# Hybrid encoder trunk on one core: a buffer for each operand of the first head pair, its V products and the tables' products in another place, and roots and reciprocals of the norms on 16 turned columns

## What is computed

```python
def rmsnorm(x, g):
    y = xf * lax.rsqrt(jnp.mean(xf * xf, axis=-1, keepdims=True) + RMS_EPS)
    return (y * g.astype(jnp.float32)).astype(x.dtype)
...
def reference(x, ...):
    for layer in range(DEPTH):
        h = rmsnorm(x, attn_norm[layer])
        if layer % 2 == 0:
            x = x + even_mixer(h, even_w_in[i], na_rpb[i], even_w_out[i], t5_table)
        else:
            x = x + mla_mixer(h, odd_w_in[i], ...)
        h = rmsnorm(x, ffn_norm[layer])
        x = x + swiglu(h, ffn_w_gate[layer], ffn_w_up[layer], ffn_w_down[layer])
    return rmsnorm(x, final_norm)
```

## Time and profile before

| | us |
|---|---|
| median of three runs (lowest, highest) | 2806.12 (2805.36, 2809.89) |
| profiled execution | 2809.95 |
| its span | 2808.1 |
| TensorE busy | 2699.4 |
| DVE, POOL, ScalarE busy | 1757.6, 1435.2, 943.5 |
| mean granted clock of TensorE | 0.988 |

### The profile page before, as it was taken

The page is one execution under the profiler, slowest core; times in us unless marked ns, Lnnn a source line. Parts: engine busy times, 40 slices in busy tenths (PEclk is TensorE's granted clock), DMA queues, the critical chain, the costliest instruction groups (busy, mean ns, idle before and its releaser), DMA issues. The chain is left out here.

```text
span 2808.1 us, 41204 instructions
## 1 busy us (share of the span) xinstructions
PE 2699.4 (96%) x13500; PEld 2245.7 (80%) x13500; DVE 1757.6 (63%) x2843; ACT 943.5 (34%) x1746; POOL 1435.2 (51%) x1353
## 2 busy tenths in 40 slices
PE   6999999989999999999998999999999999999996
PEld 4888888878788887887767888888887788878875
DVE  5666666664855555555577777777566545555555
ACT  3555544562411000011235666666532001111002
POOL 2333344465656555656643333333766555665554
PEclk8999999999999999999999999999999999999998
DMA  5433334334312111111235333334432111111112
GB/s 163 109 95 91 85 77 106 90 123 138 90 46 60 52 45 49 52 56 45 69 96 138 97 88 99 92 87 142 136 98 61 49 49 60 45 57 55 45 45 75
DMA packets 273210, 228.43 MB, mean 81 GB/s; under 512 B 44585, under 2 KB 237473, under 8 KB 272897
## 3 DMA queue, kind: packets, MB, share of 16 engines
q1 hardware_dynamic: 271223, 222.16, 28.4%
q10 hardware_dynamic: 1859, 4.64, 0.5%
HBM read 158.06 MB, written 17.04 MB: 62 GB/s over the span
## 5 line engine op out<-in xcount | busy, mean ns | idle before, releaser
L773 POOL TENSOR_SCALAR xT<-xT,rden 128x1024 f32<-128x1024 f32 (+2 forms) x256 | 278.0, 1086 | 645.7 <-DVE rden L1898 645.7
L814 POOL TENSOR_TENSOR ring<-block_t,ring 128x512 fp32r<-128x512 f32 x312 | 411.0, 1317 | 24.9
L1176 PE MATMUL psS<-times_r,ring 128*128 128x512 f32 x928 | 366.6, 395 | 16.0 <-ACT rstd L1589 9.5
L812 POOL CAST ring<-block_t 128x512 fp32r<-128x512 f32 x312 | 208.8, 669 | 322.1 <-PE psD L1210 138.3
L1483 ACT ACTIVATE pt<-psD 128x512 fp32r<-128x512 f32 (+2 forms) x512 | 257.9, 557 | 337.5 <-PE psD L985 336.5
L1177 PE MATMUL psS<-times_r,ring 128*128 128x512 f32 x928 | 363.3, 391 | 0.0
L1178 PE MATMUL psS<-times_r,ring 128*128 128x512 f32 x928 | 363.1, 391 | 0.0
L1906 DVE TENSOR_TENSOR pt<-psD,pt 128x512 fp32r<-128x512 f32 (+2 forms) x512 | 303.8, 635 | 81.3 <-ACT pt L1483 80.7
L2097 DVE TENSOR_TENSOR xT<-psD,xT 128x512 f32<-128x512 f32 x320 | 218.8, 690 | 175.1 <-PE psD L1210 175.1
L1890 DVE CUSTOM_DVE_ANT_0 xT<-psS,xT 128x1024 f32<-128x1024 f32 (+2 forms) x256 | 287.5, 1123 | 4.3 <-PE psS L972 3.4
L1472 ACT ACTIVATE xT<-xT,mneg 128x1024 f32<-128x1024 f32 (+2 forms) x256 | 273.5, 1069 | 35.6 <-DVE mneg L1890 35.3
(11 more groups left out here) (288 smaller groups left out, 5005.2 us busy)
## 6 DMA issues: line engine op xcount, KB each, us to landing
block_t<-in_w_gate SPq DMA_DIRECT2D x96, 256.0 KB, 2.9
block_t<-in_w_up SPq DMA_DIRECT2D x96, 256.0 KB, 3.3
block_t<-in_w_down SPq DMA_DIRECT2D x88, 256.0 KB, 3.1
kq<-split_x SPq DMA_DIRECT2D x126, 128.0 KB, 2.4
kq<-row SPq DMA_DIRECT2D x126, 128.0 KB, 2.3
xT<-rel_c SPq DMA_DIRECT2D x16, 960.0 KB, 5.3
stage<-in_w_even SPq DMA_DIRECT2D x24, 512.0 KB, 3.8
heads<-o_out SPq DMA_DIRECT2D x128, 64.0 KB, 2.1
```

What stands on the lines that cost most here:

```text
L773: pool.tensor_scalar(s, s, rden[:, t % 4:t % 4 + 1], 1.0, ALU.mult, ALU.mult).then_inc(S["normed"], 1)
L814: pool.tensor_tensor(lo, src, hi.bitcast(F32), ALU.subtract).then_inc(S["ws"], 1)
L1176: pe.matmul(o, unit(u, 0)[:, w], hi, start=first and k == 0, stop=False)
```

## The change

- `split_buf` and `even_bank`: in the first pair every operand has its own buffer (n = 1, 2, 3 in parts of `pt`, which the first tile's probabilities overwrite later) and every product its own bank.
- `move_even` takes the heads to move: all four operands of head 0 are moved ahead of those of head 1. Tile 0 waits for 10 DMAs, tile 4 for the other Q half of head 0, tile 8 for head 1; the first `keep_p_hi` waits for all 24.
- The tables' products stand after the fourth step of the first projection (`first_tables`), and ScalarE copies them after its sixth square. The mean products follow the whole K and Q projection, and both V products follow the means, ahead of the scores; their multiplies by the norm follow the last eviction on DVE.
- Norms: DVE transposes the bank of means in blocks of 32 x 32 (`turn_means`). Since all partitions hold the same means, every 32nd column then holds all that is needed. ScalarE takes the root of these 16 columns (`narrow_root`), DVE the reciprocal, and transposes 16 blocks of 32 repeated columns back (`narrow_reciprocal`). All norms are made so.
- In the last norm the eighth square of part 0 is added by POOL, so its mean is one product; turn, root and reciprocal are placed between the sums of tiles 11 to 15, and the second part's chain between the products of the first part. The two parts' multipliers have a bank each.

In the core of the diff, left-out lines are marked; semaphore counts of other places are renumbered.

```diff
-            if pair == 0 and n == 2:
-                return xT[:, SEQ:2 * SEQ].rearrange("p (s t) -> p s t", s=2).bitcast(F32R)
+            if pair == 0 and n:
+                return pt[:, (1 + n) * SEQ:(2 + n) * SEQ].rearrange("p (s t) -> p s t", s=2)
...
         def even_bank(pair, n):
-            return psD[(0, 1, 2, 3, 0, 1)[n]] if pair == 0 else ps_p
+            if pair:
+                return ps_p
+            return psD[n] if n < 4 else psS[1][:, (n - 4) * HALF:(n - 3) * HALF]
...
+        def turned_row(h):
+            return row[:, h * HALF:(h + 1) * HALF]
+        def first_of_32(a):
+            return a[:, ::32]
...
-            def move_even(pair, n):
+            def move_even(pair, n, heads_of=(0, 1)):
                 c, h = n // 2, n % 2
-                cols, b, sem = slice(h * HALF, (h + 1) * HALF), split_buf(pair, n), S[f"ev{n % 2}"]
+                cols, b = slice(h * HALF, (h + 1) * HALF), split_buf(pair, n)
+                sem = S[f"ev{n % 2}" if pair else "m_e1" if heads_of == (1,) else "m_kq" if n < 3 else "m_q1"]
                 sp.wait_ge(S["ev_lo"], kept_even(pair, n))
-                for e in range(2):
+                for e in heads_of:
                     q, kh, kl = even_ops(2 * pair + e)
...
-            for n in range(4):
-                move_even(0, n)
+            for e in range(2):
+                for n in range(4):
+                    move_even(0, n, (e,))
...
-            def add_squares(ph, part):
+            def add_squares(ph, part, n=KT - 1):
                 h = 1 - part
-                for j in range(1, KT - 1):
+                for j in range(1, n):
...
-                add_squares("last", part)
+                add_squares("last", part, KT - part)
...
+            def first_tables():
+                pe.wait_ge(S["toh"], 48)
+                pe.wait_ge(S["setup"], 5)
+                for c in range(4):
+                    mm = pe.matmul(psS[c // 2][0:48, (c % 2) * HALF:(c % 2 + 1) * HALF], xT[0:33, T5E:T5E + 48],
+                                   xT[0:33, ONEHOT + c * HALF:ONEHOT + (c + 1) * HALF], start=True, stop=True)
+                mm.then_inc(S["tv"], 1)
             for k in range(KT + 1):
                 if k < KT:
                     first_quarter(0, k)
                 if k:
                     first_quarter(1, k - 1)
-                if k == KT - 1:
-                    pe.wait_ge(S["tc"], at("load", "tc", 2))
-                    pe.wait_ge(S["a_add"], KT - 1)
-                    for h in range(2):
-                        pe.matmul(psS[0][:, h * HALF:(h + 1) * HALF], ones[:, :], rstd[:, h * HALF:(h + 1) * HALF],
-                                  start=True, stop=True).then_inc(S["a_ms"], 1)
+                if k == 3:
+                    first_tables()
+            pe.wait_ge(S["tc"], at("load", "tc", 2))
+            pe.wait_ge(S["a_add"], KT - 1)
+            pe.wait_ge(S["setup"], 5)
+            for h in range(2):
+                pe.matmul(psS[0][:, h * HALF:(h + 1) * HALF], ones[:, :], rstd[:, h * HALF:(h + 1) * HALF],
+                          start=True, stop=True).then_inc(S["ms"], 1)
             pe.wait_ge(S["const"], 32)
-            for part in range(2):
-                even_product(0, 4, part)
+            for n in (4, 5):
+                even_product(0, n, 0)
+                even_product(0, n, 1)
             for t in range(-1, TILES + 3):
...
                 if t + 1 < TILES:
                     nxt = (t + 1) // NSTEP
-                    if (t + 1) % NSTEP == 0:
-                        pe.wait_ge(S["ev0"], 16 * 12 * (nxt + 1))
-                        pe.wait_ge(S["ev1"], 16 * (12 * nxt + 8))
+                    if t < 0:
+                        pe.wait_ge(S["turn"], at("norm_a0", "turn", 2))
+                        pe.wait_ge(S["m_kq"], 16 * 10)
+                    elif t == 0:
+                        pe.wait_ge(S["v_row"], 2)
+                    elif t + 1 == 4:
+                        pe.wait_ge(S["m_q1"], 16 * 2)
+                    elif t + 1 == QB:
+                        pe.wait_ge(S["m_e1"], 16 * 12)
+                    elif (t + 1) % NSTEP == 0:
+                        pe.wait_ge(S["ev0"], 16 * 12 * nxt)
+                        pe.wait_ge(S["ev1"], 16 * (12 * nxt - 4))
                     elif (t + 1) % NSTEP == 4:
-                        pe.wait_ge(S["ev1"], 16 * 12 * (nxt + 1))
-                    if t < 0:
-                        pe.wait_ge(S["sr"], at("norm_a0", "sr", 2))
+                        pe.wait_ge(S["ev1"], 16 * 12 * nxt)
                     scores(0, t + 1, window_even, even_operands)
-                if t == 0:
-                    for part in range(2):
...
                 if h:
-                    pe.wait_ge(S["sr"], at(norm, "sr", 1))
...
                     if norm and n == 10:
-                        mean_of_part(norm, 0, psD[1])
+                        pe.wait_ge(S["sqm"], at(norm, "sqm", 7))
...
             ffn("ffn_1", "norm_f1")
             last_down("ffn_1", "last")
-            mean_of_part("last", 1, psD[1])
+            pe.wait_ge(S["turn"], at("last", "turn", 1))
+            pe.wait_ge(S["sqm"], at("last", "sqm", 13))
+            pe.matmul(psD[1], ones[:, :], square_place(0, 0), start=True, stop=False)
...
-                sc.activation(rstd[:, h * HALF:(h + 1) * HALF], src, ACT.Sqrt, bias=eps[:, 0:1], scale=1.0 / DM)\
-                    .then_inc(S["sr"], 1)
+            def narrow_root(ph, n, of, tiles=KT):
+                sc.wait_ge(S["turn"], at(ph, "turn", n + 1))
+                r = first_of_32(of)
+                sc.activation(r, r, ACT.Sqrt, bias=eps[:, 0:1], scale=1.0 / (tiles * P)).then_inc(S["sr"], 1)
...
+                if j == 5:
+                    sc.wait_ge(S["tv"], 1)
+                    for b in range(2):
+                        sc.activation(xT[0:48, VREL + b * SEQ:VREL + (b + 1) * SEQ], psS[b][0:48, :], ACT.Copy)\
+                            .then_inc(S["tc"], 1)
             for h in range(2):
-                sc.wait_ge(S["a_ms"], h + 1)
-                sc.activation(rstd[:, h * HALF:(h + 1) * HALF], psS[0][:, h * HALF:(h + 1) * HALF], ACT.Sqrt,
-                              bias=eps[:, 0:1], scale=1.0 / DM).then_inc(S["sr"], 1)
+                narrow_root("norm_a0", h, turned_row(h))
...
+                elif t0 == 0 and t == 0:
+                    sc.wait_ge(S["m_kq"], 16 * 10)
+                    sc.wait_ge(S["m_q1"], 16 * 2)
+                    sc.wait_ge(S["m_e1"], 16 * 12)
...
                 o = even_bank(pair, n)
                 sc.wait_ge(S["e_m"], kept_even(pair, n))
-                if pair or n != 2:
-                    sc.wait_ge(S[f"ev{h}"], 16 * (12 * pair + (8 if c else 0)))
...
+                narrow_root(ph, 1, rstd[:, HALF:SEQ])
...
                     add_squares(j)
-                if j == 2:
-                    ve.wait_ge(S["tv"], 1)
-                    for b in range(2):
-                        ve.tensor_copy(xT[0:48, VREL + b * SEQ:VREL + (b + 1) * SEQ], psS[b][0:48, :])\
...
+            def turn_means(ph, n, src, to):
+                ve.wait_ge(S["ms"], at(ph, "ms", n + 1))
+                ve.transpose(to, src).then_inc(S["turn"], 1)
+            def narrow_reciprocal(ph, n, of, to):
+                r = first_of_32(of)
+                ve.wait_ge(S["sr"], at(ph, "sr", n + 1))
+                ve.reciprocal(r, r).then_inc(S["inv"], 1)
+                ve.wait_ge(S["inv"], at(ph, "inv", n + 1))
+                ve.transpose(to.rearrange("p (b c) -> p b c", c=32),
+                             r.rearrange("p (b c) -> p b c", c=1).broadcast_to([P, HALF // 32, 32]))\
+                    .then_inc(S["rr"], 1)
+                ve.wait_ge(S["rr"], at(ph, "rr", n + 1))
             def reciprocal_half(ph, h):
-                ve.wait_ge(S["sr"], at(ph, "sr", h + 1))
-                ve.reciprocal(psD[2], rstd[:, h * HALF:(h + 1) * HALF]).then_inc(S["rr"], 1)
-                ve.wait_ge(S["rr"], at(ph, "rr", h + 1))
+                r = rstd[:, h * HALF:(h + 1) * HALF]
+                turn_means(ph, h, psD[3], r)
+                narrow_reciprocal(ph, h, r, psD[2])
             def scaled_half(ph, j, h, g):
...
             for h in range(2):
-                reciprocal("norm_a0", h, h)
+                turn_means("norm_a0", h, psS[0][:, h * HALF:(h + 1) * HALF], turned_row(h))
+            for h in range(2):
...
                     return
...
                 if t and filler_even(t - 1):
                     even_root(*filler_even(t - 1)[0:2])
...
+            def turn_latent_means(n):
+                turn_means("latent", n, psD[(1, 3, 1, 1)[n]], turned_latents(n))
             def reciprocal_of_latents(n):
-                ve.wait_ge(S["sr"], at("latent", "sr", n + 1))
-                ve.reciprocal(root_place[n], root_place[n]).then_inc(S["rr"], 1)
-                ve.wait_ge(S["rr"], at("latent", "rr", n + 1))
+                if n < 2:
```

(44 more changed lines are left out.)

90 lines of the change are left out of this document (29 added, 61 removed).

## The result

The changed kernel takes 2788.57 us (median of six runs, 2783.94 to 2796.09) against 2806.42 for the kernel before beside it (2805.36 to 2809.89): ratio 0.9939, 95% interval 0.9928 to 0.995, so 17.9 us less. Five more runs gave 2788.35, 18.7 us under the kernel before on that chip. The forecast was 26.8 us less, 2779.3, with a range of 2771 to 2792. So the measured time lies inside the range for 8 in 10, near its upper end, and outside the 2772 to 2786 that the prediction gave its stated case. The profiled execution of the changed kernel took 2787.0 us (span 2785.2), 22.9 us under the first profile of before.

The account below looks back on a forecast made before the run. TensorE, busy 2699.4 of 2808.1 us, was taken as the bound, leaving about 109 us of gaps plus clock losses. Gains 9.5 + 4.2 + 6.1 + 7.0 = 26.8 off 2806.12 gave 2779.3 us; 8-in-10 range 2771 to 2792.

Parts of the forecast that it names:

- stated case: Whole kernel: the summed gains of opening, feed-forward, latent and last norms; chance 0.50, own range 2772 to 2786 us.
- Prices: Norm chains: transposes 0.66 and 0.70 us, root 0.25, reciprocal 0.26; about 1.9 us in all, 2.1 less than before.
- the rival that needed slow transposes: Sixteen transposes on the paths make the kernel slower, decided from 2.35 us each; 2822 us at 3.36 each; chance 0.03.
- The opening: First 80 us: reordered projections, tables, moves and shorter norm chain gain 9.0 to 11.3 us; 9.5 taken.
- the first copy of probabilities ... waits for all 24 moves: Opening: this copy overwrites the move buffers, so is late next, at 66.4 to 68.7 us against 77.74 before.
- 42.8 if the clock is up at once, 45 if it must rise again: Opening: time in us when TensorE finishes the projection passes left at 20.05 and the tables' products.
- the opening gives little: Rival: clock low through idle bits and late wait for all 24 moves; gain 3 instead of 9.5, 2786 us; chance 0.22.
- gains nothing; it loses 1.4 to 3.7 us: Opening: moving the tables' products behind k = 3 makes the first mean ready at 43.7 to 46.0 us against 42.3.
- 2.1 us less reaches that Silu whole: Feed-forward second-half norm: the shorter chain brings TensorE's awaited Silu nearer by 2.1 us; 4.2 in two layers.
- u = 10: Feed-forward: a TensorE gap where 1.1 of the 2.1 us would show, the rest in the long gap.
- the 6.1 us of the sum: Latent stage near 1450 us: TensorE's gap closes, 3.1 us, and the slow run behind it goes, 3.0 more.
- Last norm: 7.0 forecast: Last norm: shorter chains start the final eight products at 2792 to 2793.5 us against 2799.59; 6.1 to 7.6, 7.0 taken.

Follow-up runs that it names:

- stage_early: Changed kernel with the loads of the next pair's weights issued before the moves instead of behind all 24; 2783.04 us, ratio 0.9917.
- opening_only: Changed kernel with feed-forward, latent and last norms as before, only the opening as changed; 2802.49 us against 2807.01 for the kernel before, ratio 0.9988.
- before_again: The kernel before, unaltered, for a second profile; 2807.52 us.
- latent_wide: Changed kernel with the latent stage's norms as before; 2794.35 us.
- again: The changed kernel unaltered, for a second profile and more times; 2788.35 us.
- both: Changed kernel with early loads of the next weights and the tables' products ahead of the projections; 2782.25 us against 2807.64 for the kernel before, ratio 0.9909.
- ffn_wide: Changed kernel with the feed-forward norms as before; 2790.06 us.

## Why the prediction came out as it did

The prediction summed to 26.8 us and 17.9 were measured: the direction and the four places were right, the sum was too large by half of what came. The largest part of the miss is the opening, and the wide range took it in. By the times, each against the kernel before of its own series, the parts are: opening 4.5, feed-forward norms 2.2, latent 5.4, last norm 6.7. They sum to 18.8, where the whole change gave 18.7. That they meet so closely is luck: by the intervals of the ratios, taken as independent, the opening is uncertain by some 3 us and each other part, a difference of two ratios, by some 5. The leads bear out the order of size, except for the latent part, as said below.

**Prices: right.** The 16 transposes that lie on paths took 0.69 to 0.73 us (forecast 0.66 and 0.70), the narrow root 0.33 (0.25), the reciprocal of 16 columns 0.21 to 0.26 (0.26). In the feed-forward norm DVE's last scaled tile lies 2.0 us nearer (739.52 against 729.68, less the lead of 7.86), where 2.1 was forecast. The one element per cycle and lane of the Trainium skill ("Vector Engine (DVE) Microarchitecture Reference", 3.8), about 0.55 us by the prediction's estimate, has no fixed part in it: with the 0.16 us of the earlier trace rows it makes 0.71, which the traces have. So the rival that needed slow transposes had nothing to stand on.

**The opening: 9.5 forecast, 4.5 measured; the chain right, the sum twice too large.** First projection at 11.59 (11.8), first move at 51.03 (49.3 to 51.6), tile 0 at 59.35 (57.4 to 59.7), probability copy at 68.85 (66.4 to 68.7): 8.9 us, where 9.0 to 11.3 were forecast. Two steps then failed. First, "the first copy of probabilities ... waits for all 24 moves" was taken as the last late thing, but SP's queue behind the moves holds the next weights' load, and POOL in its own order waits for it ahead of tile 2: 3.2 to 4.5 us lost by mark 97, shown by stage_early. This is the walk past every queue that the prediction made for the table stores and not for this load. Second, "42.8 if the clock is up at once, 45 if it must rise again" allowed for one rise. In three of eight profiles the low level lasted 6.8 us, in two of these the clock fell once more after it, and the first mean product started anywhere from 43.1 to 49.2 us. In the seven profiles with this opening and SP's order the lead at mark 97 was 5.6, 4.3, 5.5, 1.6, 3.0, 3.7 and 0.5, 3.5 on average. So the rival *the opening gives little*, "full clock isn't held through the three idle bits", with its gain of 3, was nearer than the stated case, though its reason was only half of it, as it knew nothing of POOL's wait; that the tables' move alone "gains nothing; it loses 1.4 to 3.7 us" was right as far as it went (2.4 us in the profile).

**Feed-forward norms: 4.2 forecast, 2.2 measured.** The step "2.1 us less reaches that Silu whole" failed: 0.7 us of the 2.0 went to the block in between, 27.75 us long instead of 27.07. TensorE's wait for the Silu copy shrank from 4.7 to 4.4, and the gap of 0.7 that the prediction calls u = 10 went. The first profile's lead shows 2.2 and 2.6, but part of that is a shorter fall of the clock (3.4 us for 6.8 in before), which opening_only has in the first layer with the old norm too. The effect of SBUF was not in the prediction at all.

**Latent: 6.1 forecast, 5.4 measured by the times, 3.2 to 6.3 by the profiles.** DVE's evictions came 5.3 us nearer (1453.10 against 1437.32, less the lead of 10.5) instead of 4.0, and no wait for POOL is left at that product:

```profile
1437.32 1.28 DVE L2175 TENSOR_TENSOR raw_t<-psS,rstd 128x512 f32<-128x512 f32 x2
...
1444.19 1.02 PE L1303 MATMUL psD<-block_t,ones 128*128 128x512 f32 x2
```

In the first profile the lead grows by exactly the 6.1 us of the sum, 3.1 for the gap and 3.0 for the low clock; that the clock's part was there to be won is luck of the two profiles compared. What the sum had as certain is not: the low clock behind the gap lasted 6.8, 6.8, 3.4 and 0 us in four profiles with the old norms (before, before_again, opening_only, latent_wide), and their leads grow 6.1, 6.3, 5.5 and 3.2 us less there than the changed kernel's.

**Last norm: 7.0 forecast, 6.7 measured** (6.3 in the profile's lead, forecast range 6.1 to 7.6). The eight products started at 2776.59, with a wait of 2.5 us for POOL's sums. The prediction's own times leave 1.2 us of it (POOL's last sum at 2786.6, TensorE's last tile at 2791.63 - 6.21 = 2785.42). DVE kept pace, as the prediction said; POOL's last three adds ran without a break from 2765.98 to 2770.11:

```profile
2770.26 1.61 PE L1411 MATMUL psD<-rstd,ones 128*128 128x512 f32 x2 [2.45 <-POOL rstd L883]
...
2776.59 5.35 DVE L2313 SCALAR_TENSOR_TENSOR xT<-xT,gain,psS 128x512 f32<-128x512 f32 x8
```

## What to carry to other kernels

When transfers are packed ahead of others in one queue, follow what is queued behind them to its first reader and what stands behind that reader on its engine: here two loads, moved ahead of the moves, were worth 3 to 5 us. An early start is worth little to TensorE where it runs dry behind it: four products in front, with work joined on behind them, beat an earlier start followed by 3.2 us of idle, by 2.4 us at the first mean and 1.6 in the median. And a chain that gets shorter shifts what follows against the other engines: here, where DVE and GpSimd both read SBUF, 0.7 of 2.0 us was lost again.

## What the runs showed of the hardware

A gap of about 3 us of TensorE does not have one price. Behind the latent gap of 3.0 to 3.7 us the low clock lasted 0, 3.4 or 6.8 us in different kernels. Behind the wait of 2.5 to 2.9 us ahead of the last quarter of the first feed-forward stage it lasted 3.4 us in all fourteen profiles; behind the same wait in the second one it lasted 3.4 us in eleven and did not fall in three (again, both, ffn_wide). Around the idle bit at 20 us it lasted 3.4 or 6.8. So an estimate that closes a gap should count the gap as sure and the clock as a chance. Two queues issuing moves at once raised the issue time from 0.60 to as much as 1.13 us each and lengthened TensorE's wait for the first queue's moves by 1.8 us (four moves beside them) and 3.3 us (twelve).
